# A decoder kernel on one core: a head's scaling behind the first item of the weight refill

## The reference, cut to what matters

```python
p = jax.nn.softmax(logits, axis=-1)              # mla: 8 heads; fox: 8 heads with a forget gate
o = jnp.einsum('bhqk,bkhd->bqhd', p, v)

a = p[0] - lam * p[1]                            # diff: 8 heads, two maps each
o = rmsnorm_2(a @ v, subln_w) * (1.0 - lam_init)

p = jax.nn.softmax(sc, axis=-1)                  # moba: 16 heads
```

## Time and profile before

| | us |
|---|---|
| median of 3 runs | 996.29 (996.22 to 997.15) |
| the profiled execution | 996.0 |
| its span, first to last instruction | 994.2 |
| TensorE matmuls busy | 985.5 (99%) |
| TensorE weight loads busy | 887.9 (89%) |
| VectorE busy | 718.0 (72%) |
| ScalarE busy | 599.3 (60%) |
| chain that ended last | TensorE 76%, VectorE 14%, ScalarE 6% |
| DMA | 196.72 MB, mean 198 GB/s |

### The profile page before, as it was taken

The page is one execution under the profiler, slowest core; times in us unless marked ns, Lnnn a source line. Parts: engine busy times, 40 slices in busy tenths (PEclk is TensorE's granted clock), DMA queues, the critical chain, the costliest instruction groups (busy, mean ns, idle before and its releaser), DMA issues.

```text
span 994.2 us, 16644 instructions
## 1 busy us (share of the span) xinstructions
PE 985.5 (99%) x6636; PEld 887.9 (89%) x6636; DVE 718.0 (72%) x1221; ACT 599.3 (60%) x1018; POOL 0.4 (0%) x5
## 2 busy tenths in 40 slices
PE   9999999999999999999999999999999999999997
PEld 7899999998888888999999888888999899888886
DVE  5898888878888888977668656665766458565552
ACT  4778656557665656867747545455666446555452
POOL 0000000000000000000000000000000000000000
PEclk9999999999999999999999999999999999999999
DMA  9975768545556664563336655565553327555521
GB/s 367 405 251 179 264 224 303 197 147 212 206 185 245 216 249 170 212 213 128 128 117 222 207 193 194 173 207 195 217 183 129 128 106 257 204 174 181 204 82 42
DMA packets 28443, 196.72 MB, mean 198 GB/s; under 512 B 3152, under 2 KB 3664, under 8 KB 5584
## 3 DMA queue, kind: packets, MB, share of 16 engines
q1 hardware_dynamic: 28224, 195.41, 55.3%
q10 hardware_dynamic: 144, 0.26, 0.1%
HBM read 194.61 MB, written 1.05 MB: 197 GB/s over the span
## 4 chain that ended last, share of the span: by engine, by line
PE 76%; DVE 14%; ACT 6%; issue 2%; DMA 1%; SPq 0%; DVEq 0%; ACTq 0%
PE PS L1393 16%; PE PS L1280 10%; PE PS L1080 8%; PE PS L1081 7%; PE PS L1082 7%; DVE wlo L1964 7%; PE PS L1284 5%; PE PS L1233 3%; PE PS L1236 3%; PE PS L1234 3%; ACT whi L1555 2%; ACT PB L1848 2%; PE PS L1314 2%; DVE PB L2440 2%; PE PS L1315 2%
## 5 line engine op out<-in xcount | busy, mean ns | idle before, releaser
L1964 DVE TENSOR_TENSOR wlo<-raw,whi 128x1024 fp32r<-128x1024 f32 x306 | 358.4, 1217 | 58.9 <-ACT whi L1555 56.1
L1555 ACT ACTIVATE whi<-raw 128x1024 fp32r<-128x1024 f32 x300 | 297.9, 1047 | 58.4 <-PE PS L1393 52.8
L1280 PE MATMUL PS<-HX,whi 128*128 128x512 f32 x736 | 230.9, 395 | 0.0
L1284 PEld LDWEIGHTS PS<-HX,wlo 128*128 128x128 f32 x736 | 138.2, 188 | 32.3
L1080 PE MATMUL PS<-HX,whi 128*128 128x256 f32 x496 | 145.1, 292 | 0.4 <-DVE HX L1938 0.4
L1284 PE MATMUL PS<-HX,wlo 128*128 128x256 f32 x736 | 144.6, 278 | 0.0
L1081 PE MATMUL PS<-HX,whi 128*128 128x256 f32 x496 | 140.2, 283 | 0.0
L1082 PE MATMUL PS<-HX,wlo 128*128 128x256 f32 x496 | 140.1, 282 | 0.0
L1280 PEld LDWEIGHTS PS<-HX,whi 128*128 128x128 f32 x736 | 114.4, 189 | 2.6
L1080 PEld LDWEIGHTS PS<-HX,whi 128*128 128x128 f32 x496 | 94.8, 191 | 5.9 <-issue 4.3
L1081 PEld LDWEIGHTS PS<-HX,whi 128*128 128x128 f32 x496 | 95.0, 191 | 0.2
(11 more groups left out here) (285 smaller groups left out, 1813.2 us busy)
## 6 DMA issues: line engine op xcount, KB each, us to landing
raw<-wall SPq DMA_DIRECT2D x151, 1024.0 KB, 5.0
raw<-wada SPq DMA_DIRECT2D x18, 1024.0 KB, 5.0
raw<-wall SPq DMA_DIRECT2D x8, 512.0 KB, 17.0
GA<-wada SPq DMA_DIRECT2D x2, 1024.0 KB, 21.7
GA<-alibi SPq DMA_DIRECT2D x1, 2048.0 KB, 9.3
raw<-wall SPq DMA_DIRECT2D x2, 768.0 KB, 5.9
X<-xt SPq DMA_DIRECT2D x1, 1024.0 KB, 5.1
KM<-wada SPq DMA_DIRECT2D x1, 1024.0 KB, 14.5
```

The source lines that it names most:

```text
L1280: e.matmul(PS[:, b + nt, :], whi[place(n)][:, at + nt * 128:at + nt * 128 + 128], HX[:, k, :, :].rearrange("p h t -> p (h t)"), start=k == ...
L1284: m = e.matmul(PS[:, b + nt, 0:T], wlo[place(n)][:, at + nt * 128:at + nt * 128 + 128], Hh[:, k, :], start=False, stop=k == 7, skip_group_ ...
L1555: e.activation(whi[place(n)][:, c], raw[i % RAW][:, c], ACT.Copy).then_inc(*up("a_whi", (n, half)))
L1964: e.tensor_tensor(wlo[place(n)][:, c], raw[i % RAW][:, c], f32(whi[place(n)][:, c]), ALU.subtract).then_inc(*up("v_wlo", (n, half)))
```

## The change

`ensure` and `refill` get a second argument, a function to be called once: `ensure` calls it behind the first item (and its load), or at its end if there was no item; `refill` calls it ahead of a pending `ada_sum` if there is one. `rows` hands `after` to `refill` once any head exists. `tokens`, `wide`, `together` and the steps written out by hand are as before.

```diff
-    def ensure(n):
+    def ensure(n, after_one=None):
         while st["next"] < len(ITEMS) and st["have"] < n:
...
             taken(i)
+            if after_one:
+                after_one()
+                after_one = None
+        if after_one:
+            after_one()
...
-    def refill(n):
+    def refill(n, after_one=None):
         if late_sums and late_sums[0][0] <= n:
+            if after_one:
+                after_one()
+                after_one = None
             ada_sum(late_sums.pop(0)[1])
-        ensure(n + HL + (n + HL + 1 >= MORE_FROM))
+        ensure(n + HL + (n + HL + 1 >= MORE_FROM), after_one)
...
             evac(n, b, pr)
-        after()
-        if fill:
-            refill(n)
+        if fill and heads["all"]:
+            refill(n, after)
+        else:
+            after()
+            if fill:
+                refill(n)
```

## The result

| | before | after |
|---|---|---|
| median (range, runs) | 996.33 us (996.22 to 997.15, 4) | 1014.94 us (1013.69 to 1016.67, 4) |
| ratio, 95% interval | | 1.0186 [1.0174, 1.0198] |
| the profiled execution, its span | 996.0, 994.2 | 1016.7, 1014.5 |

The change makes the kernel 18.6 us slower. Forecast were 13.2 us, so the sign was right and the size was not: 1014.9 lies above the range of 1006 to 1013. What follows looks for the missing 5.4 us.

The account below looks back on a forecast made before the run. TensorE was taken to pace every head stage, so late VectorE results only cost: 0.6 + 9.9 + 2.65 = 13.2 us on the profiled 996.0 gave 1009.2, and 0.29 for the median made 1009.5, range 1006 to 1013.

Parts of the forecast that it names:

- TensorE paces the head stages: All head stages: TensorE has almost no waits there, so a faster VectorE has nothing to give.
- The rival with 988 us: Fox and mla: VectorE's filled idle, 6 x 1.38 = 8.3 us, comes back, if nothing stalls in diff; chance 2%.
- Fox and mla, 0.6: Four of six moved scales cost nothing; fox 3 and mla 3 make TensorE 0.25 and 0.38 us late.
- Diff, 9.9: Second block's first attention stage: five stalls of TensorE, 10.3 us from late scales and sub-norm steps, less 0.45.
- Diff 0, diff 2 and diff 5: Heads of diff whose transposes wait for the scale behind rounding and split: 2.86, 1.30 and 2.20 us late.
- the credit of 0.45: Taken off diff's 10.3 us: late exponentials catch up and diff 4's wait goes; ends at 0 and 1.5.
- diff 4's wait: Existing 0.2 us wait of TensorE at diff 4, which was to go as part of the 0.45 taken off.
- Moba, 2.65: Moba stage: late transposes at moba 0, 3 and 5 cost 1.35, 0.62 and 0.68 us; moba 2 nothing.
- The drained table load, 8%: Rival: a drain of about 1.38 us per moved table load, or handoffs that add up: 1011 to 1016; 8%.
- The clock falls, 4%: Rival: TensorE drops to 1.2 GHz behind each of five diff stalls, 5 x 2.9 = 14 us, 1024; 4%.
- its own signs of being wrong: Diff longer by less than 5, fox and mla shorter, or granted clock leaving 1.00 in a head stage.
- The range: Whole kernel: 1006 to 1013, from the reduces' start, the credit, handoffs and table load, widened towards drained load and absorbed stalls.

Follow-up runs that it names:

- e1_first: Moved order in the fox and mla stage only, against the kernel before: 996.97 us, ratio 1.0004.
- e9_free: Moved order only at fox 2, mla 0 to 2 and moba 2, against the kernel before: 996.40 us, ratio 1.0001.
- e5_warm: Changed kernel plus matmuls that nobody reads ahead of the five waiting groups in diff: 1010.23 us, ratio 1.0137 to the kernel before.
- e3_moba: Moved order in the moba stage only, against the kernel before: 999.20 us, ratio 1.0027.
- e8_sums1: Only the second sub-norm step (sub_sums) moved behind the split, no scale with it, against the kernel before: 998.96 us, ratio 1.0025.
- e4_sums_ahead: Changed kernel, but the pending sub-norm step stays ahead of the refill and only the scale moves: 1008.73 us, ratio 1.0124 to the kernel before.
- e6_diff0: Only diff 0's scale moved behind the split, against the kernel before: 1001.37 us, ratio 1.0045.
- e2_diff: Moved order in the diff stage only, against the kernel before: 1012.56 us, ratio 1.0153.

## Why the forecast had the sign and missed the size

- *TensorE paces the head stages, so VectorE's filled idle time is worth nothing:* right. e1_first and e9_free fill it and stay within 0.05% of before. The rival with 988 us is out.
- *Fox and mla, 0.6:* right, 0.73 in the trace and 0.5 in e1_first.
- *Diff, 9.9:* right for what it named. Stall by stall the trace has 10.1, and e5_warm, at full clock, 10.1. Diff 0, diff 2 and diff 5 came within 0.05 us of their sums. Of the credit of 0.45 some 0.25 showed: diff 4's wait is gone (0.13) and diff 3 is 0.1 shorter.
- *Moba, 2.65:* right, 2.67 in the trace and 2.7 in e3_moba, with nothing for moba 2.
- *The drained table load, 8%:* wrong. By the section "What ACT_TABLE_LOAD costs" of the Trainium skill's "ScalarE: Activation LUTs" each of the two moved loads would have cost 1.38 us more; in the trace of e8_sums1 its user follows 1.29 us after the load's start, as in the trace of before (452.70 and 453.99), and the transposes came within 0.07 us of the sum without a drain.
- *The clock falls, 4%, argued away and put at nothing in the sum:* this is the step that failed. It said that "at the end of the kernel it has no matmul for 4 us and the granted clock stays at 1.00; my longest stall is 2.9 us". The earlier trace rows is a window *inside* a gap, with no matmul behind it. In the changed kernel too the clock reads 1.00 inside the gaps (434 to 436.5) and falls once work is back. (In e4_sums_ahead it fell 2.0 us into a gap, so a fall inside is possible; that a gap shows none says nothing of what follows.) In the trace of before the clock does fall, 4.8 us after the last matmul (988.94 to 993.78), at the very end of the span, where nothing could pay for it any more; the windows are these:

```profile
988.00:989.00 1.00, 0.94 (x5) 0.44 (x3) 1.00 (x4) 0.33 (x3) 0.00 (x0) 1.00 0.00 0
...
993.50:994.20 0.70, 0.00 (x0) 0.00 (x0) 0.00 (x0) 0.00 (x0) 0.00 (x0) 0.70 0.00 0
```

  The row answered another question than the one put to it. e5_warm prices the clock at 4.7 us of the median, the trace at 6.0 in its execution; the forecast without it is met by e5_warm, 1010.2 against 1009.5. The rival itself was too dear, with five falls at 2.9 us: there were three, and they cost 2.95, 1.5 and 1.5. Of its own signs of being wrong the prediction had named the right one, the granted clock leaving 1.00 in a head stage. The Trainium skill, "TensorE: Matmul & The Clock Gate", section "HAM oscillation — how this bites in real kernels", warned of this kind of loss; here the traces agree with it in kind (0.92 over the diff stage).
- *The range:* its sources were handoffs and the reduces, errors of tenths (they add up to 1007.0 at the low end, not 1006.5). It ended at 1013 because the one term worth several us had been given 4% and no room.

Left open is what decides whether a given gap brings the fall. It came behind 2.3 us in the changed kernel and, by time and mean clock, in four of five executions of e6_diff0, behind 1.84 us twice in the profiled execution of the change, once in that of e2_diff and at most once in ten in e8_sums1, and not behind 1.74 us at diff 5. Two executions of e4_sums_ahead, which has a gap of 2.3 and one of 2.0 us, show a mean clock of 1.000. The 2.2 us by which e4_sums_ahead shrinks the stalls rest on the trace of one execution.

## What to carry to other kernels

Where one engine already paces a stage, filling another engine's idle time was worth nothing here, and a reorder on that other engine could only cost. Price it by following one chain from its first waiting instruction to the pacing engine, and compare the start of the same instruction in both traces, since waits shown in brackets miss the stalls inside a group. A forecast that opens gaps of a few us in a saturated TensorE must carry the clock as a term with its own range, and evidence for or against it must be a gap with matmuls *behind* it. If such a gap can't be avoided, matmuls that nobody reads can fill it: here they took back 4.9 of 18.6 us.

## What was not expected of the hardware

- The granted clock mostly falls after the work has come back. Of the eight falls in diff in the traces here (three in the change, two each in e2_diff and e4_sums_ahead, one in e6_diff0) seven came 0.3 to 1.7 us after it: behind the first sub-norm's gap (464 to 465.9 us) at 467.5, in e6_diff0, where work came back at 435.7, about 1 us later. One, in e4_sums_ahead, came 0.3 us ahead of it, in the gap.
- It stays down for 3.4 us (six of the eight falls) or 6.8 us, with matmuls of 256 columns 0.213 us apart instead of 0.12 (0.56 of the rate, not half), and the profile shows TensorE fully busy then. A rise of its busy time with the same instructions is a sign to look for, though not all of it is the clock (6.0 of 10.2 us here in diff).
- It isn't the same in each execution: four runs of the change span 3.0 us, those of e4_sums_ahead 4.4, and those of e5_warm, where the gaps are filled, 1.2.
